# Second attention of a two-block transformer kernel: normalised weights, value products by feature, rounding straight from PSUM

## The chip, the cores and the metric

One NeuronCore of a Trainium2 chip runs the whole program in one launch. The metric is device time in microseconds (us), the median of the runs. Three runs of the kernel before took 1004.45, 1004.01 and 1004.02 us.

## The reference

Two transformer blocks run one after the other on 256 tokens of width 1024, all in float32. The first has an FFN, a mixer of two attentions, and another FFN. The second has an HGRN2 mixer beside a softmax attention of 8 heads of 128 features (called MoBA; with 256 tokens there is a single block, so it is plain causal attention with a relative bias), then a merge of the two branches, an output projection and an FFN. The change touches this attention alone. What it computes, for each head:

```
lo = einsum('bhqd,bhsd->bhqs', qc, ko) * Dh ** -0.5
lo = where(dist_o >= 0, lo + table_h[:, t5_bucket(dist_o)], -inf)
p = softmax(lo, axis=-1)
o = einsum('bhqs,bhsd->bhqd', p, vo)
```

and later `o @ w_branch_attn`, a product over the 1024 features of all heads.

## The kernel before

**Products at full precision.** Every large product with weights is done in a rounded 32-bit format (float32r). Each operand is split into a rounded part (hi) and the rest (lo), and the product is three matmuls: hi by hi, hi by lo, lo by hi (`three`). One such group over 128 rows of the inner dimension is called a tile here: 3 matmuls of 128x512. A `half` is four tiles. A weight piece (128x2048, 1 MB) serves two halves, one for each 128 tokens (t = 0, 1), and PE waits for the piece (`lo_ready`) at the first tile of its first half. A piece takes three steps: two DMAs bring it into one of three slots of `raw`, issued once the lo part of the piece three places before is made; ScalarE (ACT) writes its hi part (`hi`, L1258); VectorE (DVE) writes the lo part by subtraction (`lo`, L1870; `half_lo`, L1876, does it in two instructions, and signals with the second).

**Attention beside a projection.** The second block's projection (36 pieces, `N_WIN2`) is still running when the attention starts. `attention_between` exists once for each engine, and each engine does its own list in order, so the order in the code is the order of the work. Eight heads are taken as four pairs p = 8 to 11. For each pair PE does: `scores` (waits for q, k and `o_out`, the output of the pair before, since scores and outputs share the PSUM tensor `gu`), some tiles of the projection, `turn_weights` (six transposes of the exponentials), more tiles, `weights_read` (waits until the transposed weights are copied to SBUF), `turn_qk` for the next pair, `values`, and the last tiles. `laid` says how many tiles stand in the three places: before the change (4, 1, 2) quarters, which is 8, 2 and 4 tiles.

DVE's list in a pair: `maxima` (adds the bias, finds row maxima), the lo parts of pieces put off, a PSUM evacuation where a block of the projection has ended, `weights_out` (copies the transposed weights), `also` (the gate product of the HGRN2 branch, `gate_of`, for pairs 9 and 10), `k_out`, `output` (four products with the reciprocal of the softmax sum, from PSUM to `proj`), one more lo part. ACT's list: `exps`, hi parts and evacuations, `weights_out`, `q_out`.

**Value products.** The transposed weights are the stationary operand, the values move, and the output has tokens on its partitions (three 128x128 matmuls a head, L948 to L950, each in float32, which the trace records as two matmuls).

**Into operand form.** The product with `w_branch_attn` (T_WAT, four pieces from N_WAT) needs the features on the partitions. So in the stage of the HGRN2 branch product (T_WHG) PE turns the outputs back, 16 transposes in four fills (L654), DVE copies them out (`fill_scaled`, L1888), ACT rounds them (L1268) and DVE subtracts (`fill_rest`, L1896).

Of the kernel before, what the change touches and what calls it, by code (L numbers as in the profile page):

```python
# [7 lines left out]
F32 = mybir.dt.float32  # L8
# [51 lines left out]
TURN_AFTER = {T_WOUT: N_WOUT, T_WAT: N_WHG, T_WOUT2: N_WAT}  # L60
# [15 lines left out]
FOX_LEAD = (3, 3)  # L76
FOX_BEHIND = {4: (1, 2), 5: (1, 2), 6: (1, 1), 7: (0, 0)}
# [46 lines left out]
def build(nc, x_d, wg_d, wu_d, wd_d, win_d, wout_d, win2_d, whg_d, wat_d, wout2_d,  # L124
          fixed_d, rows_d, post_d, rel_d, level_d, hot_d, out_d, row_d, skew_d):

    with ExitStack() as ctx:
# [117 lines left out]
        late_exp, late_rden, o_first = sem("late_exp"), sem("late_rden"), sem("o_first")  # L245
        pT_full, pT_a, pT_d, pv_done, o_out = sem("pT_full"), sem("pT_a"), sem("pT_d"), sem("pv_done"), sem("o_out")
# [93 lines left out]
        def laid(p, q0):  # L340


            behind = (4, 1, 2)
            q = q0 + 2 + sum(behind) * (p % 4)
            out = []
            for n in behind:
                out.append(list(range(q, q + n)))
                q += n
            if p % 4 == 3:
                out[2] = []  # L350
            return out

        def halves(quarters):

            return [q // 2 for q in quarters if q % 2]
# [16 lines left out]
        def fill_bank(u, i):  # L372

            if u == T_WOUT:
                return (gu if i < 2 else acc[:, 1, :, :])[:, i % 2, :]
            return {T_FFN2: acc[:, 1, :, :], T_WHG: acc[:, 1, :, :], T_WAT: gu, T_WOUT2: gu}.get(u, tp)[:, i % 2, :]
# [34 lines left out]
        def turn_n(u):  # L411
            return 4 * u
# [195 lines left out]
        def _(pe):  # L608
# [8 lines left out]
            def half(k, r, banks, j, t, u=None, tiles=range(4), first_j=0, after_first=None):  # L617

                if t == 0 and tiles[0] == 0:
                    pe.wait_ge(lo_ready, k + 1 + 3 * r)  # L620
                w_hi, w_lo = (w.rearrange("p (k n) -> p k n", k=4) for w in split_weights(k))
                for a in tiles:
                    hi, lo = (place[:, a, :] for place in turned_place(u, t, j))
# [19 lines left out]
            def quarters(n0, g0, qs):  # L643
                for q in qs:
                    block_half(n0, g0, q // 2, range(2 * (q % 2), 2 * (q % 2) + 2))
# [447 lines left out]
            def attention_between(p0, n0, g0, h0):  # L1093
# [3 lines left out]
                for p in range(p0, p0 + 4):  # L1097
                    here = laid(p, 2 * h0)
                    scores(p)
                    quarters(n0, g0, here[0])  # L1100
                    turn_weights(p)
                    quarters(n0, g0, here[1])
# [4 lines left out]
                    quarters(n0, g0, here[2])  # L1107
# [99 lines left out]
            for j in range(2):  # L1207
                for t in range(TT):
                    half(N_WHG + 2 + j, 0, acc[:, :, 1, :], j, t, T_WHG)
                    if (j, t) == (0, 1):  # L1210
                        pe.wait_ge(o_out, 12)
                        fills(T_WAT, from_proj(AQ), 0, 1)
                    elif (j, t) == (1, 0):
                        fills(T_WAT, from_proj(AQ), 2, 3)

            filled(T_WAT, 4)
            for j in range(2):
                for t in range(TT):
                    half(N_WAT + j, 0, gu, j, t)
            pe.wait_ge(evac_a, 24)  # L1220
            pe.wait_ge(evac_d, 24)
            for j in range(2):
                for t in range(TT):
# [3 lines left out]
                    half(N_WAT + 2 + j, 0, tp, j, t)  # L1227
# [22 lines left out]
        def _(act):  # L1250
# [164 lines left out]
            def exps(p):  # L1415
# [5 lines left out]
                if pair(p)[0] == 1:  # L1421
                    n = 4 * (p % 2)
                    for r, part in enumerate((late_half, early_half)):
                        cols = slice(S, 3 * P) if r else slice(0, S)
                        for h in range(2):
                            at = 2 * r + h
                            ins = act.activation(e_sb[:, h, cols], part(p, h), ACT.Exp, bias=nmx[:, n + at:n + at + 1],
                                                 accum_out=den[:, at:at + 1])
                        ins.then_inc(exp_done if r else late_exp, 1)
                    return  # L1430
                for h in range(2):
                    lt = late_half(p, h) if p < 8 else src[:, h, 0:S]
                    el = early_half(p, h) if p < 8 else src[:, h, S:3 * P]
# [77 lines left out]

            def attention_between(p0, n0, g0, h0):
# [4 lines left out]
                for p in range(p0, p0 + 4):  # L1517
                    here = [halves(q) for q in laid(p, 2 * h0)]
# [203 lines left out]
            fills(T_WAT, 0, 1, 2, 3)  # L1722
# [134 lines left out]
        def _(dve):  # L1857
# [254 lines left out]
            def weights_out(p):  # L2112
# [8 lines left out]
                reciprocals(p)  # L2121

            def mix(p):

                n = 6 * (p % 2)
                dve.wait_ge(late_exp, p + 1)
                dve.reciprocal(rden[:, n:n + 2], den[:, 0:2]).then_inc(late_rden, 1)
                dve.wait_ge(late_rden, p + 1)
# [111 lines left out]
            def attention_between(p0, n0, g0, h0, also=lambda p: None):  # L2240

                block_out(n0, g0, h0 - 1)
                k_out(p0)
                put_off = [h0 - 1]
                for p in range(p0, p0 + 4):
                    here = [[h for h in halves(q) if h % 2] for q in laid(p, 2 * h0)]
# [13 lines left out]
                    output(p)  # L2260
                    if p < p0 + 3 and put_off:
# [295 lines left out]
            def gate_of(p):  # L2557

                t = p - 8
# [35 lines left out]
            fills(T_WAT, 0, 1, 2, 3)  # L2595
# [84 lines left out]
```

## Time and profile before

| | us |
|---|---|
| median of three runs | 1004.02 |
| the profiled execution, its own time | 1004.47 |
| its span, first to last instruction | 1002.7 |
| PE busy | 997.2 |
| DVE busy | 709.0 |
| ACT busy | 488.2 |

The profile is of one execution. Its page gives busy times, the chain of work that ended last and the costliest groups; the trace behind it gives each instruction in order of time, what ended each wait, and the busy time of any stretch. The engines are PE (matmuls), PEld (loads of the stationary operand), DVE, ACT, POOL and SP. The attention of the change lies between 683 and 746 us of the span, and the products with the two branches' weights between 746 and 790.

### The profile page before, as it was taken

The numbers are of one execution on the slowest core, as the hardware profiler recorded it, in microseconds if no ns is written. First come the engines' busy times: TensorE is split into PE (matmuls) and PEld (weight loads), VectorE is DVE, ScalarE is ACT, GpSimd is POOL, SyncE is SP. The second block draws the span as 40 slices with busy tenths as digits, with TensorE's granted clock in tenths as the row PEclk, the third lists the DMA queues.
The fourth block names the chain that finished last, engine by engine and source line by source line (L and its number), as shares of the span: only waits on it lengthen the run. The fifth ranks groups of instructions, "written<-read, shape, count | busy, mean of one in ns | idle before, by whom it ended". The sixth has DMA issues, their size and how long they took to land.

```text
span 1002.7 us, 14623 instructions
## 1 busy us (share of the span) xinstructions
PE 997.2 (99%) x5311; PEld 838.0 (84%) x5311; DVE 709.0 (71%) x818; ACT 488.2 (49%) x614; POOL 209.9 (21%) x205
## 2 busy tenths in 40 slices
PE   9999999999999999999999999999999999999998
PEld 6888888878888888888888888888888888888887
DVE  5876767775788767666764479876877777666664
ACT  6444444664665544444544455466446445434342
POOL 2232222014100232323010081151000012313230
PEclk9999999999999999999999999999999999999999
DMA  9655656745424655465736545344535556555551
GB/s 301 231 176 186 207 183 204 258 134 182 127 91 162 206 172 209 168 209 167 266 133 209 171 166 166 129 145 149 168 116 180 167 169 222 174 192 192 186 207 43
DMA packets 116937, 178.53 MB, mean 178 GB/s; under 512 B 5792, under 2 KB 73920, under 8 KB 116768
## 3 DMA queue, kind: packets, MB, share of 16 engines
q1 hardware_dynamic: 115952, 174.86, 51.9%
q0 software_dynamic: 640, 1.42, 0.5%
q10 hardware_dynamic: 304, 1.70, 0.5%
q8 instruction: 27, 0.44, 0.2%
q14 instruction: 14, 0.11, 0.0%
HBM read 176.88 MB, written 2.64 MB: 179 GB/s over the span
## 4 chain that ended last, share of the span: by engine, by line
PE 95%; DVE 2%; DMA 1%; SPq 1%; ACT 1%; issue 1%; POOL 0%; DVEq 0%
PE acc L611 11%; PE acc L615 11%; PE acc L614 11%; PE tp L791 10%; PE gu L791 10%; PE gu L794 5%; PE tp L794 5%; PE tp L611 4%; PE tp L615 4%; PE tp L614 4%; PE gu L611 3%; PE gu L615 3%; PE gu L614 3%; PE acc L1056 1%; DMA raw<-in_gate 1%; PE acc L879 1%
## 5 line engine op out<-in xcount | busy, mean ns | idle before, releaser
L1870 DVE TENSOR_TENSOR wlo<-raw,whi 128x2048 fp32r<-128x2048 f32 x144 | 339.8, 2368 | 156.0 <-ACT whi L1258 155.2
L1258 ACT ACTIVATE whi<-raw 128x2048 fp32r<-128x2048 f32 x150 | 285.7, 1907 | 55.4 <-PE acc L615 22.2
L791 PE MATMUL tp<-act_in,whi 128*128 128x512 f32 x432 | 103.0, 391 | 0.0
L791 PE MATMUL gu<-act_in,whi 128*128 128x512 f32 x432 | 102.6, 390 | 0.0
L1778 POOL TENSOR_TENSOR tmp<-tmp 128x256 f32<-128x256 f32 x54 | 41.9, 775 | 280.8 <-DVE tmp L1989 280.8
L791 PEld LDWEIGHTS gu<-act_in,whi 128*128 128x128 f32 x432 | 80.9, 188 | 16.6
L611 PE MATMUL acc<-whi,hT_hi 128*128 128x512 f32 x240 | 94.1, 392 | 0.0
L1780 POOL TENSOR_TENSOR sil<-sil,tmp 128x256 f32<-128x256 f32 x54 | 86.9, 1608 | 34.0 <-ACT sil L1330 34.0
L614 PE MATMUL acc<-wlo,hT_hi 128*128 128x512 f32 x240 | 93.7, 390 | 0.0
L615 PE MATMUL acc<-whi,hT_lo 128*128 128x512 f32 x240 | 93.4, 389 | 0.0
L791 PEld LDWEIGHTS tp<-act_in,whi 128*128 128x128 f32 x432 | 79.7, 188 | 16.2 <-DVE wlo L1870 0.5
L1335 ACT ACTIVATE hT_hi<-hid 128x256 fp32r<-128x256 f32 x54 | 22.2, 417 | 138.3 <-DVE hid L2000 131.1
L611 PE MATMUL tp<-whi,act_in 128*128 128x512 f32 x192 | 76.9, 401 | 0.0
L615 PE MATMUL tp<-whi,act_in 128*128 128x512 f32 x192 | 75.0, 391 | 0.0
L614 PE MATMUL tp<-wlo,act_in 128*128 128x512 f32 x192 | 74.8, 390 | 0.0
L1330 ACT ACTIVATE sil<-tmp 128x256 f32<-128x256 f32 x54 | 22.0, 408 | 106.4 <-POOL tmp L1778 106.4
L611 PE MATMUL acc<-whi,act_in 128*128 128x512 f32 x176 | 71.0, 403 | 0.0
L615 PE MATMUL acc<-whi,act_in 128*128 128x512 f32 x176 | 68.8, 391 | 0.0
L614 PE MATMUL acc<-wlo,act_in 128*128 128x512 f32 x176 | 68.6, 390 | 0.0
L1761 POOL TENSOR_SCALAR ms<-sums 128x1 f32<-128x1 f32 (+2 forms) x20 | 12.6, 630 | 245.7 <-ACT junk L1280 159.5
L794 PEld LDWEIGHTS tp<-act_in,wlo 128*128 128x128 f32 x432 | 55.4, 191 | 2.1
L794 PEld LDWEIGHTS gu<-act_in,wlo 128*128 128x128 f32 x432 | 55.4, 191 | 2.1
(345 smaller groups left out, 1800.5 us busy)
## 6 DMA issues: line engine op xcount, KB each, us to landing
raw<-in_w_in SPq DMA_DIRECT2D x96, 512.0 KB, 4.5
raw<-in_down SPq DMA_DIRECT2D x66, 512.0 KB, 4.1
raw<-in_gate SPq DMA_DIRECT2D x64, 512.0 KB, 4.1
raw<-in_up SPq DMA_DIRECT2D x64, 512.0 KB, 4.7
raw<-in_w_out SPq DMA_DIRECT2D x16, 512.0 KB, 4.7
raw<-in_w_branch_hg SPq DMA_DIRECT2D x8, 512.0 KB, 4.4
raw<-in_w_branch_attn SPq DMA_DIRECT2D x8, 512.0 KB, 4.7
post<-in_post_gains SPq DMA_DIRECT2D x3, 512.0 KB, 5.8
```

Source lines behind the costliest of these rows:

```text
L611: pe.matmul(out, hi, w_hi, start=start, stop=False)
L614: pe.matmul(out, hi, w_lo, start=False, stop=False)
L615: return pe.matmul(out, lo, w_hi, start=False, stop=stop)
L791: pe.matmul(banks[:, a, :], w_hi[:, i, a * P:(a + 1) * P], both, start=i == 0, stop=False)
L794: mm = pe.matmul(banks[:, a, 0:S], w_lo[:, i, a * P:(a + 1) * P], act_in[:, i, 0, :], start=False, stop=i == KT - 1)
L1258: act.activation(split_weights(k)[0], raw[:, k % RING, :], ACT.Copy).then_inc(hi_ready, 1)
L1330: act.activation(sil[:, a, :], gate[:, a, :], ACT.Silu).then_inc(sil_ready, 1)
L1335: act.activation(hT_hi[:, a, :], hid[:, a, :], ACT.Copy).then_inc(hT_hi_ready, 1)
L1761: link(pool.tensor_scalar(ms[:, 0:n], sums[:, col:col + n], inv, EPS, ALU.mult, ALU.add))
L1778: pool.tensor_tensor(gate[:, a, :], gate[:, a, :], row, ALU.mult).then_inc(gate_scaled, 1)
L1780: pool.tensor_tensor(sil[:, a, :], sil[:, a, :], row, ALU.mult).then_inc(sil_scaled, 1)
L1870: dve.tensor_tensor(w_lo, raw[:, k % RING, :], w_hi.bitcast(F32), ALU.subtract).then_inc(lo_ready, 1)
```

## The change

1. ACT's `exps` for these pairs does both heads' late queries (tokens 128 to 255, 256 columns) first and both heads' early ones (128 columns) after, and signals each part.
2. DVE gets `normed_weights`: for the late part a reciprocal and two products of 128x256 in SBUF, for the early part the same with 128x128. It stands after the evacuations and ahead of `weights_out`. The reciprocal in `weights_out` falls away.
3. PE's `turn_weights` waits for `mixed` (once for the late, once for the early part), and places the early block first.
4. `values`: the values are the stationary operand, the weights move. A head takes one matmul of 128x256 and one of 128x128; the output has features on its partitions.
5. The output leaves PSUM as an operand: ACT writes the hi part (`rounded_out`, 128x512, placed after `q_out`), DVE the lo part (`output`, one subtraction of 128x512 in place of four products). They go to the columns that the queries and keys of the same pair held.
6. The four fills of T_WAT fall away on PE, ACT and DVE; its halves take their stationary operand from there (`stationary`).
7. The tiles stand 9, 2, 3 (9, 1, 0 for the last pair) in place of 8, 2, 4.
8. The lo part of the piece that was put off from the pair before is done in two instructions: the first where the whole stood, the second after `output`.
9. `gate_of` comes one pair earlier: its first call before the maxima of pair 8, its second in pair 9.

```diff
@@ constants
+MOBA_BEHIND, MOBA_LAST = (9, 2, 3), (9, 1, 0)
@@ laid
-            behind = (4, 1, 2)
-            q = q0 + 2 + sum(behind) * (p % 4)
+            q = 4 * h0 + 4 + sum(MOBA_BEHIND) * (p % 4)
...
+            for n in MOBA_BEHIND if p % 4 < 3 else MOBA_LAST:
@@ operands
+        def stationary(u, t, j, a):
+            if u == T_WAT:
+                return [place(2 * j + a // 2)[:, a % 2, t * P:(t + 1) * P] for place in (attn_hi, attn_lo)]
+            return [place[:, a, :] for place in turned_place(u, t, j)]
@@ PE turn_weights
+                if pair(p)[0] == 2:
+                    for r, blocks in enumerate(((0, 1), (2,))):
+                        pe.wait_ge(mixed, 2 * mixed_n(p) + r + 1)
+                        for h in range(2):
+                            for n in blocks:
+                                to = (n + 1) % 3 * P
+                                mm = pe.transpose(turned[:, h, to:to + P], e_sb[:, h, n * P:(n + 1) * P], idn)
+                    mm.then_inc(pT_full, 1)
+                    return
@@ PE values
+                    if kind == 2:
+                        o = gu[:, 0, h * S:(h + 1) * S]
+                        pe.matmul(o, v[0], pT_sb[:, h, 0:S], start=True, stop=False, skip_group_check=True)
+                        mm = pe.matmul(o[:, P:S], v[1], pT_sb[:, h, S:3 * P], start=False, stop=True, skip_group_check=True)
+                        continue
@@ PE, products with the branch weights
-                    if (j, t) == (0, 1):
-                        pe.wait_ge(o_out, 12)
-                        fills(T_WAT, from_proj(AQ), 0, 1)
-                    elif (j, t) == (1, 0):
-                        fills(T_WAT, from_proj(AQ), 2, 3)
-            filled(T_WAT, 4)
+            pe.wait_ge(o_out, 12)
-                    half(N_WAT + j, 0, gu, j, t)
+                    half(N_WAT + j, 0, gu, j, t, T_WAT)
@@ ACT
+            def rounded_out(p):
+                act.wait_ge(pv_done, p + 1)
+                act.activation(attn_hi(p - 8), heads(gu[:, 0, :], 2), ACT.Copy).then_inc(attn_hi_ready, 1)
...
                     if p < p0 + 3:
                         q_out(p + 1)
+                    rounded_out(p)
...
-            fills(T_WAT, 0, 1, 2, 3)
@@ DVE
+            def late_reciprocals(p):
+                n = 6 * (p % 2)
+                dve.wait_ge(late_exp, mixed_n(p) + 1)
+                dve.reciprocal(rden[:, n:n + 2], den[:, 0:2]).then_inc(late_rden, 1)
+                dve.wait_ge(late_rden, mixed_n(p) + 1)
+            def normed_weights(p):
+                n = 6 * (p % 2)
+                late_reciprocals(p)
+                for h in range(2):
+                    e = e_sb[:, h, 0:S]
+                    ins = dve.tensor_scalar(e, e, rden[:, n + h:n + h + 1], None, ALU.mult)
+                ins.then_inc(mixed, 1)
+                dve.wait_ge(exp_done, p + 1)
+                dve.reciprocal(rden[:, n + 2:n + 4], den[:, 2:4]).then_inc(rden_ready, 1)
+                dve.wait_ge(rden_ready, p + 1)
+                for h in range(2):
+                    e = e_sb[:, h, S:3 * P]
+                    ins = dve.tensor_scalar(e, e, rden[:, n + 2 + h:n + 3 + h], None, ALU.mult)
+                ins.then_inc(mixed, 1)
@@ DVE output
+                if kind == 2:
+                    dve.wait_ge(attn_hi_ready, i + 1)
+                    dve.tensor_tensor(attn_lo(i), heads(gu[:, 0, :], 2), attn_hi(i).bitcast(F32), ALU.subtract)\
+                       .then_inc(o_out, 1)
+                    return
@@ DVE attention_between
                 k_out(p0)
+                also(p0 - 1)
...
                     maxima(p)
-                    for h in put_off:
-                        next_lo(n0, g0, h)
+                    pieces = [n0 + h // 2 + RING for h in put_off]
+                    for k in pieces:
+                        half_lo(k, 0)
                     for h in here[0]:
                         block_out(n0, g0, h)
                     put_off = here[0] + here[1]
+                    normed_weights(p)
                     weights_out(p)
...
                     output(p)
+                    for k in pieces:
+                        half_lo(k, 1)
...
@@ DVE, later
-            fills(T_WAT, 0, 1, 2, 3)
@@ gate_of
-                t = p - 8
+                t = p - 7
```

## Rows read from the trace of the kernel before

**Rows 1.** The page: busy time, share of the span and instructions of each engine.

```profile
PE 997.2 (99%) x5311; PEld 838.0 (84%) x5311; DVE 709.0 (71%) x818; ACT 488.2 (49%) x614; POOL 209.9 (21%) x205
```

**Rows 2.** PE's longest wait of the whole span; then busy times from 683 to 790 us.

```profile
PE gu L675 <- DVE junk L2311: 1.2, 1, 1.2
...
683.00:790.00 107.00, 107.00 (x554) 90.71 (x553) 76.96 (x103) 55.73 (x76) 0.00 (x0) 1.00 0.45 148
```

**Rows 3.** The timeline (start, duration, engine, line): PE at two places.

```profile
745.79 0.39 PE L611 MATMUL acc<-whi,proj_rounded 128*128 128x512 f32 x1
...
762.12 1.03 PE L654 MATMUL gu<-fixed,proj 128*128 128x128 f32 x8
762.91 0.48 PE L611 MATMUL acc<-whi,proj_rounded 128*128 128x512 f32 x1
763.22 0.40 PE L614 MATMUL acc<-wlo,proj_rounded 128*128 128x512 f32 x1
```

**Rows 4.** The timeline: PE in pair 8, and the scores of pair 9.

```profile
688.10 0.48 PE L611 MATMUL acc<-whi,act_in 128*128 128x512 f32 x1
...
693.68 0.82 PE L936 MATMUL acc<-fixed,att_e 128*128 128x128 f32 x6
...
694.25 0.48 PE L611 MATMUL acc<-whi,act_in 128*128 128x512 f32 x1
...
696.60 0.39 PE L948 MATMUL gu<-proj,att_pT 128*128 128x128 f32 x2
...
697.86 0.47 PE L611 MATMUL acc<-whi,act_in 128*128 128x512 f32 x1
...
699.33 0.40 PE L611 MATMUL tp<-whi,act_in 128*128 128x512 f32 x1
...
700.71 0.59 PE L917 MATMUL gu<-att_k,att_q 128*128 128x256 f32 x2
...
701.93 0.48 PE L611 MATMUL tp<-whi,act_in 128*128 128x512 f32 x1
```

**Rows 5.** The timeline: DVE in pair 8 (idle before it, in brackets).

```profile
688.38 0.76 DVE L2097 SCALAR_TENSOR_TENSOR tmp<-gu,proj 128x256 f32<-128x256 f32 x2 [3.29 <-PE gu L920]
...
690.62 2.28 DVE L1870 TENSOR_TENSOR wlo<-raw,whi 128x2048 fp32r<-128x2048 f32 x1
...
698.14 1.13 DVE L2160 TENSOR_SCALAR proj<-gu,rden 128x128 f32<-128x128 f32 x4 [0.59 <-PE gu L950]
...
701.38 0.74 DVE L2051 TENSOR_SCALAR proj<-acc,rstd 128x512 f32<-128x512 f32 x1
```

**Rows 6.** The timeline: ACT in pairs 8 and 11, and PE's values of pair 11.

```profile
690.75 0.51 ACT L1435 ACTIVATE att_e<-tmp,nmx 128x256 f32<-128x256 f32 x1 [3.92 <-DVE nmx L2110]
...
696.80 0.69 ACT L1412 ACTIVATE att_q<-acc,fixed 128x512 f32<-128x512 f32 x1 [1.78 <-PE acc L879]
...
734.57 1.90 ACT L1258 ACTIVATE whi<-raw 128x2048 fp32r<-128x2048 f32 x1
736.38 0.47 ACT L1446 ACTIVATE att_pT<-acc 128x384 f32<-128x384 f32 x1
...
737.20 0.38 PE L948 MATMUL gu<-proj,att_pT 128*128 128x128 f32 x2
```

**Rows 7.** Groups of DVE instructions by shape: count, busy us, mean ns, idle before.

```profile
L1896 DVE TENSOR_TENSOR act_in<-tmp,act_in 128x512 fp32r<-128x512 f32 x26 | 17.7, 690 | 11.7 <-ACT act_in L1268 11.6
...
L1876 DVE TENSOR_TENSOR wlo<-raw,whi 128x1024 fp32r<-128x1024 f32 x12 | 14.5, 1217 | 0.0
...
L2563 DVE TENSOR_TENSOR proj<-proj 128x1024 f32<-128x1024 f32 x2 | 2.4, 1194 | 0.0
...
L2140 DVE SCALAR_TENSOR_TENSOR att_e<-att_e,rden 128x256 f32<-128x256 f32 x4 | 1.9, 486 | 0.1
...
L2170 DVE TENSOR_SCALAR proj<-proj,rstd 128x128 f32<-128x128 f32 x8 | 1.8, 279 | 0.0
...
L2127 DVE RECIPROCAL rden<-den 128x2 f32<-128x2 f32 x4 | 0.7, 162 | 1.1 <-ACT att_e L1427 1.1
```

More of the change, by code:

```diff
@@ L59 @@
 T_FFN1, T_WIN, T_WOUT, T_FFN2, T_WIN2, T_WHG, T_WAT, T_WOUT2, T_FFN3 = range(9)
-TURN_AFTER = {T_WOUT: N_WOUT, T_WAT: N_WHG, T_WOUT2: N_WAT}
+TURN_AFTER = {T_WOUT: N_WOUT, T_WOUT2: N_WAT}
 BY_TILE, BY_HALF = [(0, 0), (0, 1), (1, 0), (1, 1)], [(0, 0), (1, 0), (0, 1), (1, 1)]
@@ L245, in build @@
         late_exp, late_rden, o_first = sem("late_exp"), sem("late_rden"), sem("o_first")
+        attn_hi_ready = sem("attn_hi_ready")
         pT_full, pT_a, pT_d, pv_done, o_out = sem("pT_full"), sem("pT_a"), sem("pT_d"), sem("pv_done"), sem("o_out")
@@ L338, in total, with laid, halves, mixed_n @@
             return wout_banks(b)[:, t, :] if m == 1 else acc[:, t, b, :]
-        def laid(p, q0):
-            behind = (4, 1, 2)
-            q = q0 + 2 + sum(behind) * (p % 4)
+        def laid(p, h0):
+            q = 4 * h0 + 4 + sum(MOBA_BEHIND) * (p % 4)
             out = []
-            for n in behind:
+            for n in MOBA_BEHIND if p % 4 < 3 else MOBA_LAST:
                 out.append(list(range(q, q + n)))
                 q += n
-            if p % 4 == 3:
-                out[2] = []
-            return out
-        def halves(quarters):
-            return [q // 2 for q in quarters if q % 2]
+            return out
+        def halves(tiles):
+            return [q // 4 for q in tiles if q % 4 == 3]
+        def mixed_n(p):
+            return p - (4 if p >= 8 else 0)
+        def attn_hi(i):
+            return proj_rounded[:, :, AQ + i * S:AQ + (i + 1) * S]
+        def attn_lo(i):
+            return proj_rounded[:, :, AK + i * S:AK + (i + 1) * S]
         def logits(p):
@@ L375, in fill_bank @@
                 return (gu if i < 2 else acc[:, 1, :, :])[:, i % 2, :]
-            return {T_FFN2: acc[:, 1, :, :], T_WHG: acc[:, 1, :, :], T_WAT: gu, T_WOUT2: gu}.get(u, tp)[:, i % 2, :]
+            return {T_FFN2: acc[:, 1, :, :], T_WHG: acc[:, 1, :, :], T_WOUT2: gu}.get(u, tp)[:, i % 2, :]
         def first_bank(i, a):
@@ L622, in half @@
                 for a in tiles:
-                    hi, lo = (place[:, a, :] for place in turned_place(u, t, j))
+                    hi, lo = stationary(u, t, j, a)
                     mm = three(banks[:, t, :], hi, lo,
@@ L641, in block_half, with tiles_of @@
                 half(n0 + h // 2, 0, block_banks(g), h // 2 % 2, h % 2, tiles=tiles)
-            def quarters(n0, g0, qs):
+            def tiles_of(n0, g0, qs):
                 for q in qs:
-                    block_half(n0, g0, q // 2, range(2 * (q % 2), 2 * (q % 2) + 2))
+                    block_half(n0, g0, q // 4, [q % 4])
             def fill(u, i, src):
@@ L1097, in attention_between @@
                 for p in range(p0, p0 + 4):
-                    here = laid(p, 2 * h0)
+                    here = laid(p, h0)
                     scores(p)
-                    quarters(n0, g0, here[0])
+                    tiles_of(n0, g0, here[0])
                     turn_weights(p)
-                    quarters(n0, g0, here[1])
+                    tiles_of(n0, g0, here[1])
                     weights_read(p)
@@ L1106, in attention_between @@
                     values(p)
-                    quarters(n0, g0, here[2])
+                    tiles_of(n0, g0, here[2])
             first_block()
@@ L1226, in _ @@
                         fills(T_WOUT2, from_proj(HI), 0, 1)
-                    half(N_WAT + 2 + j, 0, tp, j, t)
+                    half(N_WAT + 2 + j, 0, tp, j, t, T_WAT)
             pe.wait_ge(merged, 2 * TT)
@@ L1420, in exps @@
                 src = logits(p)
-                if pair(p)[0] == 1:
+                if pair(p)[0]:
                     n = 4 * (p % 2)
@@ L1426, in exps @@
                             at = 2 * r + h
-                            ins = act.activation(e_sb[:, h, cols], part(p, h), ACT.Exp, bias=nmx[:, n + at:n + at + 1],
-                                                 accum_out=den[:, at:at + 1])
+                            ins = act.activation(e_sb[:, h, cols], part(p, h) if p < 8 else src[:, h, cols], ACT.Exp,
+                                                 bias=nmx[:, n + at:n + at + 1], accum_out=den[:, at:at + 1])
                         ins.then_inc(exp_done if r else late_exp, 1)
@@ L1517, in attention_between @@
                 for p in range(p0, p0 + 4):
-                    here = [halves(q) for q in laid(p, 2 * h0)]
+                    here = [halves(q) for q in laid(p, h0)]
                     exps(p)
@@ L2120, in weights_out @@
                 dve.tensor_copy(pT_sb[:, 1, :], turned[:, 1, 0:3 * P]).then_inc(pT_d, 1)
-                reciprocals(p)
+                if pair(p)[0] == 0:
+                    reciprocals(p)
+            def late_reciprocals(p):
[17 more added lines that the diff above has]
+                ins.then_inc(mixed, 1)
             def mix(p):
                 n = 6 * (p % 2)
-                dve.wait_ge(late_exp, p + 1)
-                dve.reciprocal(rden[:, n:n + 2], den[:, 0:2]).then_inc(late_rden, 1)
-                dve.wait_ge(late_rden, p + 1)
+                late_reciprocals(p)
                 mix_rows(n + 4, den[:, 0:1], rden[:, n + 1:n + 2], slice(0, S), 2 * p + 1)
@@ L2243, in attention_between @@
                 k_out(p0)
+                also(p0 - 1)
                 put_off = [h0 - 1]
                 for p in range(p0, p0 + 4):
-                    here = [[h for h in halves(q) if h % 2] for q in laid(p, 2 * h0)]
+                    here = [[h for h in halves(q) if h % 2] for q in laid(p, h0)]
                     maxima(p)
-                    for h in put_off:
-                        next_lo(n0, g0, h)
+                    pieces = [n0 + h // 2 + RING for h in put_off]
+                    for k in pieces:
+                        half_lo(k, 0)
                     for h in here[0]:
```

5 lines of the change are left out of this document (2 added, 3 removed).

## The prediction

> **What bounds the kernel now.** I read the page's busy times first: PE is busy for 997.2 us of a span of 1002.7 [rows 1]. Then PE's waits over the whole span: the longest is 1.2 us, at the start, and from 683 to 790 us, where every edit lies, PE is busy for 107.00 of 107.00 us at a granted clock of 1.00, with DVE at 76.96 and ACT at 55.73 [rows 2]. So PE's queue is the time. A PE instruction removed is gained in full unless a wait takes its place, and any wait for DVE or ACT is lost in full. The third view is the timeline of PE, DVE and ACT in this stretch, since the question is whether each result is there when PE comes to it.
>
> **What PE no longer does.** The fills of T_WAT: 16 transposes in two groups of 8. One group starts at 762.12 and the next product at 762.91, and that product's follower comes after 0.31 us where 0.23 is the pace, so a group costs 0.79 + 0.08 = 0.87 us, two cost 1.75 [rows 3]. No PE wait is there to come back [rows 2]. The value products of a pair: six 128x128 matmuls from 696.60 to 697.86, 1.26 us [rows 4]. The new form, 128x256 and 128x128 for each of two heads, is the shape of the scores, 700.71 to 701.93 = 1.22 us [rows 4]. Fewer instructions, then, but as many columns: 0.04 a pair, 0.15 in all. Transposes, tiles and places between them stay equal in number. Together PE loses 1.9 us of work.
>
> **What DVE and ACT do otherwise.** DVE for each pair: the lo part of the output, one 128x512 at 0.69 [rows 7], for four products of 1.13 [rows 5]; and the normalisation. A 128x128 product in SBUF is 0.28, a reciprocal 0.16 [rows 7]. The 128x256 product in SBUF is in no row: the two-input form of that size bounds it above at 0.49, the 128x128 below at 0.28 [rows 7]. I take 0.37, near the one-input row. With about 0.03 us between dependent instructions the normalisation takes 2 x 0.2 + 2 x 0.29 + 2 x 0.2 = 1.4 us of DVE. The Trainium skill's page "VectorE: DVE Perf Modes", section "The perf-mode tier table", has float32 products with a scalar at twice the rate where both sides lie in SBUF. By that the 128x256 would take 0.28 + 0.07 = 0.35, an estimate, and the sum below would fall by under 0.1. ACT gains one rounding of 128x512 per pair, 0.69 as `q_out` of that size [rows 6]. The first gate product (two 128x1024, the first 1.19 [rows 7], so 2.3 with overlap) goes into DVE's 3.29 us of idle before the maxima of pair 8 [rows 5] and costs nothing; were that idle gone, it would cost the maxima up to 2.3. The removed fills free 5 us of DVE and 2.4 of ACT in a stage where neither holds PE, worth nothing.
>
> **Where PE will wait.** I walked the three queues instruction by instruction with the rows' durations: a tile 0.68 (0.77 right after transposes or float32 products, 697.86 to 699.33 being 0.77 + 0.70 [rows 4]), 0.28 us from a PE group's end to DVE's or ACT's start (697.86 to 698.14 [rows 4, 5]), 0.1 from a DVE end to PE, which no row shows (zero to 0.2), and 0.08 of overlap between neighbours on DVE and ACT (734.57 + 1.90 against 736.38 [rows 6]). Done so for the kernel before, the walk puts the scores of pair 9 at 700.75, where the row has 700.71 [rows 4], and finds no wait. For the kernel after it finds three.
>
> *Pair 8, the second half of a lo part.* The put-off piece is 30 of the projection, used from half 60, tile 240. Before, its lo part ran whole from 690.62 [rows 5] and PE came to that tile at 699.33 [rows 4]. Now its second instruction stands behind `output`, which waits for ACT's rounding, which waits for the values. And tile 240 still stands in the third place of pair 8 (tiles 239, 240, 241), ahead of the next scores. Nine tiles in place of eight let the values end 0.7 later, at 698.5. From there: 0.28 + 0.69 (ACT) + 0.04 + 0.61 (lo of the output) + 1.22 (second half lo [rows 7]) + 0.14 = 701.5. PE comes to tile 240 one tile (0.77) after the values, at 699.3. It waits 2.2 us. Behind that tile are queued two tiles and the scores of pair 9, so everything moves. The next load into that slot is issued 8.5 us later than before; its piece (33) isn't touched by ACT until 711.7, so that is hidden.
>
> In pair 9 the piece is 32, first used by tile 256, after the scores of pair 10; these wait for the same output, and take as long (1.22) as the half lo. No wait, though only 0.1 to 0.6 us is left.
>
> *Pair 10, the chain to the transposes.* After the output of pair 9 DVE has the half lo, a whole lo (2.28) and an evacuation (0.74) ahead of the maxima [rows 5, 7]: 716.2 to 720.2, while the scores end at 717.9. Maxima 2.24 (688.38 to 690.62 [rows 5]), 0.13 to ACT, two exponentials of 0.5 [rows 6], reciprocal and two products: the late weights are ready at 724.5. PE has nine tiles, 6.3 us, and is there at 724.2: it waits 0.4, and 0.2 more for the early weights. Before, eight tiles (688.10 to 693.68 [rows 4]) were more than enough, since exponentials were all.
>
> *Pair 11, ACT's order.* ACT's `weights_out` stands behind the exponentials, an evacuation and a hi part (1.90). Before, it started at 736.38, right behind that hi part, and PE's values at 737.20 [rows 6], so its slack was about 0.3 us. Now the maxima are held by half a lo and a whole one (733.9, scores done at 732.3), the exponentials start at 736.2, the copy at 740.4, and is read at 741.0. PE is there at 739.9: it waits 1.1.
>
> **Sum.** 2.2 + 0.6 + 1.1 = 3.9 us of waits, less 1.9 of work: 2.0 us longer. From the profiled execution's 1004.47 that is 1006.5; the median of the runs is 0.45 lower, so 1006.0. With the 128x256 product at 0.49 the waits grow to 4.0, at 0.28 they fall to 3.7. With half a microsecond either way for the second and the third, which hang on slacks of tenths, the case spans 1005.2 to 1007.0.
>
> **Rivals.** (a) *The waits are covered and the removed work is the result:* 1004.0 - 1.9 = 1002.1, faster. It would need the 2.2 us of pair 8 to vanish, so that the lo part of piece 30 is ready by 699.3; it decides where values, rounding and subtraction together take under 0.8 us, and rows 5 to 7 have 1.3 for the last two alone. Against it, then, is nearly everything; for it, that PE has not waited once here [rows 2], so slacks may be longer than my tenths. (b) *Only the wait in pair 8 comes:* 2.2 - 1.9 = +0.3, 1004.3. Pairs 10 and 11 hang on 0.4 to 1.1 us after long chains, and any of them may be shorter. (c) *The chain grows:* the scores of pair 10 and piece 32 are also within 0.6 us, and each pair's lateness is handed on through DVE, whose queue is full in pairs 9 and 10. Another 1.5 to 2 us: 1008. (d) *PE's clock falls behind the wait.* Rows have a clock of 1.00, the 2.4 GHz level, through this stretch, with no idle in it [rows 2]; a PE idle of 2.2 us in mid kernel is in no row, the longest at the start being 1.2. At 1.2 GHz the fourteen tiles of one pair would take 9.5 us more (14 x 0.68): up to 1015. The Trainium skill's page "TensorE: Matmul & The Clock Gate", section "HAM oscillation — how this bites in real kernels", says idle gaps that are long enough put the clock back to half. The trace agrees as far as it goes.
>
> **How the numbers follow.** The forecast with three waits 0.57, (a) 0.08, (b) 0.20, (c) 0.12, (d) 0.03. A measurement here tells from no change what is over about 0.2%, 2 us. The forecast's own range lies half over 1006.03 and half under, so: slower 0.29 + 0.12 + 0.03 and a little of what I have not seen, 0.48; same 0.28 + 0.20 less a little, 0.43; faster 0.09. The range from 1002.8 to 1007.8 leaves out (a), (d) and the far part of (c).
>
> **What would show it.** In the profile after: a PE wait of about 2 us near 699.3, at the first `tp` tile after the values of pair 8, released by the half lo part on DVE; the transposes of pair 10 waiting for a DVE product on `att_e`; the values of pair 11 waiting for ACT's `att_pT`; values of a pair 1.2 us long; 16 fewer transposes; the granted clock at 1.00. The forecast is wrong if the first is absent, or if the first product with `w_branch_hg` (745.79 before [rows 3]) doesn't come 3.3 to 4.5 us later.

## The result, and the profile after

The kernel after takes 1006.05 us (median of 20 runs, 1005.53 to 1007.74), the kernel before 1004.01 (20 runs, 1003.78 to 1004.45). The ratio of the means is 1.0024, 95% interval 1.0017 to 1.0030. So the change makes the kernel slower, by 2.0 us between the medians.

The 20 runs of after stand in two groups: 11 at a mean granted clock of 1.000, 1005.53 to 1006.07 with a mean of 1005.86, and 9 at 0.998, 1006.96 to 1007.74 with a mean of 1007.23. None of the 69 runs of the kernel before whose clock is on record (those beside the experiments) is below 1.000, and the longest of its 20 runs here took 1004.45. The profiled execution took 1006.01, its span is 1004.2, and it belongs to the first group. It has to be read against the profiled 1004.47 of before: 1.54 longer.

The busy times of the page answer to [rows 1]: 32 matmul records fewer, 0.5 us less of busy PE, a longer span.

```profile
PE 996.7 (99%) x5279; PEld 836.4 (83%) x5279; DVE 708.2 (71%) x821; ACT 488.2 (49%) x614; POOL 209.3 (21%) x205
```

PE's waits over the whole span (total, times, longest) answer to [rows 2]. Two are new, each happens once, and the wait of 1.2 at the start is the old one.

```profile
PE tp L628 <- DVE wlo L1906: 1.9, 1, 1.9
PE gu L692 <- DVE junk L2373: 1.2, 1, 1.2
PE gu L975 <- ACT att_pT L1471: 0.7, 1, 0.7
```

The busy times from 683 to 790 us (PE, PEld, DVE, ACT, POOL, then the clock) show 2.74 of idle PE where there was none, at a granted clock of 1.00. This is less than the delay below: idle time counts from the modelled end of the last product, some 0.17 after the next one was due, and what is held inside a group of transposes doesn't count as idle at all. Where this text says that a group of products ends, it means the start of the product behind it, as the prediction does.

```profile
683.00:790.00 107.00, 104.26 (x515) 86.87 (x514) 74.08 (x105) 53.98 (x76) 0.00 (x0) 1.00 0.46 148
```

**Pair 8.** PE's timeline, for [rows 4] (in brackets the idle before, and what ended it):

```profile
697.79 0.60 PE L975 MATMUL gu<-att_pT,proj 128*128 128x256 f32 x2
698.22 0.38 PE L976 MATMUL gu<-att_pT,proj 128*128 128x128 f32 x2
698.36 0.48 PE L628 MATMUL acc<-whi,act_in 128*128 128x512 f32 x1
...
701.24 0.47 PE L628 MATMUL tp<-whi,act_in 128*128 128x512 f32 x1 [1.93 <-DVE wlo L1906]
```

ACT's and DVE's timelines of the same moment, for [rows 5, 6]:

```profile
698.64 0.60 ACT L1540 ACTIVATE proj_rounded<-gu 128x512 fp32r<-128x512 f32 x1 [0.62 <-PE gu L976]
```

```profile
691.93 0.62 DVE L2167 TENSOR_SCALAR att_e<-att_e,rden 128x256 f32<-128x256 f32 x2
...
699.27 0.69 DVE L2205 TENSOR_TENSOR proj_rounded<-gu,proj_rounded 128x512 fp32r<-128x512 f32 x1 [1.19 <-ACT proj_rounded L1540]
699.88 1.22 DVE L1906 TENSOR_TENSOR wlo<-raw,whi 128x1024 fp32r<-128x1024 f32 x1
```

These rows are one chain: the values end at 698.36; ACT rounds (698.64); DVE subtracts (699.27) and only then makes the second half of the lo part of piece 30 (699.88 to 701.10); tile 240 starts at 701.24. Tile 239 began at 698.36 and would have let it start 0.77 later, at 699.13. So it comes 2.1 late. The products of tile 240 itself take 0.08 more than the pace (701.24 to 702.00 by the same timeline, 0.76 where a tile takes 0.68), so the place costs 2.2 in all.

**Pairs 10 and 11.** PE at the two places, then DVE in pair 10 and ACT in pair 11:

```profile
723.72 0.39 PE L632 MATMUL acc<-whi,act_in 128*128 128x512 f32 x1
724.18 1.07 PE L956 MATMUL acc<-fixed,att_e 128*128 128x128 f32 x6
...
738.24 0.82 PE L956 MATMUL acc<-fixed,att_e 128*128 128x128 f32 x6
...
740.49 0.70 PE L975 MATMUL gu<-att_pT,proj 128*128 128x256 f32 x2 [0.73 <-ACT att_pT L1471]
```

```profile
723.51 0.62 DVE L2167 TENSOR_SCALAR att_e<-att_e,rden 128x256 f32<-128x256 f32 x2
...
724.28 0.48 DVE L2174 TENSOR_SCALAR att_e<-att_e,rden 128x128 f32<-128x128 f32 x2
```

```profile
738.16 1.90 ACT L1284 ACTIVATE whi<-raw 128x2048 fp32r<-128x2048 f32 x1
739.96 0.47 ACT L1471 ACTIVATE att_pT<-acc 128x384 f32<-128x384 f32 x1
```

In pair 10 the transposes are due at 723.95 (723.72 + 0.23) and start at 724.18, when the late weights have just been made (723.51 + 0.62 = 724.13); and the group is 1.07 long where pair 11's is 0.82, since the early weights are made only at 724.76. Together 0.5. The view of waits has no row for this one, so a missing row doesn't mean that nothing waits for some tenths. In pair 11 the values are due 0.57 of transposes and 0.77 of a tile after 738.24: at 739.58. They start at 740.49, 0.9 late, behind a copy that stands behind a hi part; and the first of them takes 0.70 where the others take 0.60, so 1.0 in all.

**Behind them.** The first WHG product [rows 3] and the first WAT product:

```profile
749.15 0.39 PE L628 MATMUL acc<-whi,proj_rounded 128*128 128x512 f32 x1
...
770.91 0.39 PE L628 MATMUL gu<-whi,proj_rounded 128*128 128x512 f32 x1
```

The first comes 3.36 later than the 745.79 of before; the second 1.54 later than before's 769.37. So between them the kernel gains 1.82, the four fills. Counted from where pair 8's queries are turned (683.26 before, 683.12 after), the first comes 3.50 later.

### The profile page after: what moved, and what is told of

It is laid out like the page before. It is cut to its first block, busy times and chain, and to the rows that moved or that the text cites. A ratio compares the mean times of both kernels' runs of the same rounds, so it can differ in the third digit from the quotient of the medians.

```text
span 1004.2 us, 14552 instructions
## 1 busy us (share of the span) xinstructions
PE 996.7 (99%) x5279; PEld 836.4 (83%) x5279; DVE 708.2 (71%) x821; ACT 488.2 (49%) x614; POOL 209.3 (21%) x205
## 4 chain that ended last, share of the span: by engine, by line
PE 94%; DVE 3%; ACT 1%; issue 1%; POOL 0%; DVEq 0%; ACTq 0%
PE acc L628 11%; PE acc L631 11%; PE acc L632 11%; PE tp L808 10%; PE gu L808 10%; PE gu L811 5%; PE tp L811 5%; PE tp L628 4%; PE tp L632 4%; PE tp L631 4%; PE gu L628 3%; PE gu L631 3%; PE gu L632 3%; PE acc L1087 1%; PE acc L896 1%
## 5 line engine op out<-in xcount | busy, mean ns | idle before, releaser
L1900 DVE TENSOR_TENSOR wlo<-raw,whi 128x2048 fp32r<-128x2048 f32 x141 | 332.7, 2367 | 157.7 <-ACT whi L1284 156.8
L1808 POOL TENSOR_TENSOR tmp<-tmp 128x256 f32<-128x256 f32 x54 | 39.8, 737 | 281.6 <-DVE tmp L2019 281.6
L628 PE MATMUL tp<-whi,act_in 128*128 128x512 f32 x176 | 70.6, 401 | 1.9 <-DVE wlo L1906 1.9
L632 PE MATMUL tp<-whi,act_in 128*128 128x512 f32 x176 | 68.7, 390 | 0.0
L631 PE MATMUL tp<-wlo,act_in 128*128 128x512 f32 x176 | 68.6, 390 | 0.0
```

Of the source, the lines that this page charges most:

```text
L628: pe.matmul(out, hi, w_hi, start=start, stop=False)
L631: pe.matmul(out, hi, w_lo, start=False, stop=False)
L632: return pe.matmul(out, lo, w_hi, start=False, stop=stop)
L1808: pool.tensor_tensor(gate[:, a, :], gate[:, a, :], row, ALU.mult).then_inc(gate_scaled, 1)
L1900: dve.tensor_tensor(w_lo, raw[:, k % RING, :], w_hi.bitcast(F32), ALU.subtract).then_inc(lo_ready, 1)
```

## The experiments

Times are medians. Unless said otherwise the runs are all at a clock of 1.000. The before beside them took 1003.97 (33 runs, with E1 to E4), 1004.01 (27 runs, with E5 to E8) and 1004.17 (9 runs, with E9).

One thing has to be known before times of two traces are compared. Pair 8's queries are turned at 682.5 to 682.8 in some executions (E1, E2, E5 to E9) and at 683.1 to 683.3 in others (before, after, E3, E4). This half microsecond has nothing to do with the edits: it is there within the first 9 us of the span. So the stretch from that turn to the first WHG product is given too, where it says more than the time: 62.53 us before, 66.03 after.

**E1: piece 30 whole again.** The kernel after, with one edit in DVE's list of pair 8.

```diff
+                    whole = pieces if p == p0 else []
+                    pieces = [] if p == p0 else pieces
...
                     weights_out(p)
+                    for k in whole:
+                        lo(k)
```

> The kernel after, with one thing taken back: the lo part of piece 30, in pair 8, is done in one instruction behind DVE's weights_out, where DVE is idle for 1.7 us, instead of half of it behind output. Theory (the wait at tile 240 is that half instruction standing behind the rounding): the PE wait of 1.9 us near 699 is gone, tile 240 starts one tile (0.78) after the values, the waits of pairs 10 and 11 (0.5 and 1.0 us) stay as they are, and the time falls by 2.1 us, from 1005.9 to 1003.8. Rival (DVE's full queue in pairs 9 and 10 is the bound, the wait in pair 8 only shows it early): the time comes back as longer waits in pairs 10 and 11, fall under 1 us. On the clock: of 20 runs of the kernel after, 12 had a mean granted clock of 1.000 and took 1005.5 to 1006.1, 8 had 0.998 and took 1007.0 to 1007.7, none of the 20 before had 0.998. If the long wait is what makes the clock fall, no run of this kernel has 0.998.

(The two groups count 11 and 9, not 12 and 8.) Measured 1003.42 (11 runs, 1003.15 to 1003.99), ratio 0.9994 [0.9985, 1.0003]. That is 2.4 under the mean of after's full-clock runs; the stretch from the turn of pair 8's queries to the first WHG product is 63.86, 2.2 shorter. Its timeline of PE shows three tiles in a row behind the values, with nothing between them:

```profile
697.88 0.48 PE L628 MATMUL acc<-whi,act_in 128*128 128x512 f32 x1
...
698.66 0.39 PE L628 MATMUL tp<-whi,act_in 128*128 128x512 f32 x1
```

while its waits still hold the one of pair 11, 0.7, and its transposes in pair 10 still take 1.08. So the place of half an instruction is worth more than the whole net loss, and theory and size hold.

**E2: ACT copies the weights first in pair 11.**

```diff
                     exps(p)
+                    if p == p0 + 3:
+                        weights_out(p)
...
-                    weights_out(p)
+                    if p < p0 + 3:
+                        weights_out(p)
```

> The kernel after, with ACT's weights_out of pair 11 put ahead of the evacuation and the hi part that stood in front of it. Theory (the wait of pair 11 is ACT's order): the wait of PE's values for att_pT falls from 0.7 in the trace (1.0 with the restart) to about 0.2, time 0.8 us less, 1005.1. Rival (DVE's late normalisation holds pair 11 whatever ACT does): no change, 1005.9. The wait near 699 stays, and with it some runs at a clock of 0.998.

Measured 1006.36, ratio 1.0018 [1.0009, 1.0027], in two groups: 5 runs at 1.000 with a mean of 1005.23, 6 at 0.998 with a mean of 1006.45. At the full clock that is 0.63 less than after's 1005.86, near the 0.73 of the wait row, which is gone; the values still start 0.17 after they are due. The median missed, because more than half of the runs were at the lower clock. Its profiled execution is one of these, and shows how that looks (granted clock in the third last column):

```profile
697.00:700.00 3.00, 1.71 (x10) 1.18 (x8) 1.81 (x3) 2.27 (x4) 0.00 (x0) 1.00 0.00 0
700.00:703.00 3.00, 2.36 (x7) 1.96 (x8) 3.00 (x3) 1.24 (x1) 0.00 (x0) 0.74 0.37 72
703.00:706.00 3.00, 3.00 (x13) 2.47 (x12) 1.12 (x4) 0.00 (x0) 0.00 (x0) 0.69 1.04 395
706.00:709.00 3.00, 3.00 (x15) 2.49 (x14) 2.86 (x7) 1.39 (x6) 0.00 (x0) 1.00 0.62 232
```

```profile
700.64 0.47 PE L628 MATMUL tp<-whi,act_in 128*128 128x512 f32 x1 [1.93 <-DVE wlo L1909]
...
701.41 0.60 PE L628 MATMUL tp<-whi,act_in 128*128 128x512 f32 x1
701.80 0.63 PE L631 MATMUL tp<-wlo,act_in 128*128 128x512 f32 x1
702.23 0.63 PE L632 MATMUL tp<-whi,act_in 128*128 128x512 f32 x1
702.65 1.05 PE L934 MATMUL gu<-att_k,att_q 128*128 128x256 f32 x2
...
704.96 0.48 PE L628 MATMUL tp<-whi,act_in 128*128 128x512 f32 x1
```

Products that come every 0.23 us come every 0.43 from 701.8 on, and the pace is back at 704.96: from tile 240 to there is 4.32, in the trace of after 2.67 (701.24 to 703.91). The clock was at the 1.2 GHz level for some 3 us. In this trace it cost 1.65; the groups' means are 1.2 apart.

**E3: all three waits removed by order alone.** The kernel after with E1's and E2's edits; the split kept for pair 9 only, so that the lo part of piece 34 in pair 10 is also made whole, behind DVE's `weights_out`; the whole lo part of piece 33, which stood ahead of the maxima of pair 10, made behind them (`held`); and eight tiles in place of nine ahead of the last pair's transposes.

```diff
-MOBA_BEHIND, MOBA_LAST = (9, 2, 3), (9, 1, 0)
+MOBA_BEHIND, MOBA_LAST = (9, 2, 3), (8, 2, 0)
...
+                    split = pieces if p == p0 + 1 else []
+                    whole = [] if p == p0 + 1 else pieces
...
+                    if p == p0 + 2:
+                        lo(held)
```

> The kernel after, with four moves and no work changed: piece 30 and piece 34 whole behind weights_out; piece 33 whole behind the maxima of pair 10 instead of ahead of them; ACT's weights_out of pair 11 ahead of its evacuation and hi part; the last pair's tiles 8 and 2 instead of 9 and 1. Theory (the waits are queue positions, and the work removed from PE, 1.9 us, is gained in full once they are gone): no PE wait from 683 to 790 us, the first product with w_branch_hg near 745.5 of the span, time 1004.0 - 1.9 = 1002.1, all clocks 1.000. Rival (DVE lacks time for the normalisation beside the projection, however ordered): at least one wait of half a microsecond or more is left and the time stays over 1002.8.

Measured 1002.12 (11 runs, 1001.71 to 1002.97), ratio 0.9982 [0.9973, 0.9991]: faster than both kernels. The busy times show the stretch whole again, and the timeline has the first WHG product 0.2 ahead of the 745.79 of before (0.13 of it since the turn of pair 8's queries, which is the gain of the value products):

```profile
683.00:790.00 107.00, 107.00 (x531) 90.15 (x529) 77.27 (x105) 55.66 (x76) 0.00 (x0) 1.00 0.46 148
```

```profile
745.58 0.39 PE L628 MATMUL acc<-whi,proj_rounded 128*128 128x512 f32 x1
```

This is the removed work of 1.9 with no wait, the figure of rival (a).

**E4: the split alone, on the kernel before.**

```diff
-                    for h in put_off:
-                        next_lo(n0, g0, h)
+                    pieces = [n0 + h // 2 + RING for h in put_off]
+                    for k in pieces:
+                        half_lo(k, 0)
...
                     output(p)
+                    for k in pieces:
+                        half_lo(k, 1)
```

> The kernel before, with one part of the change alone: the put-off lo part is done in two instructions, the second behind output (still four products, no rounding by ACT, no normalisation). Theory: the split alone makes PE wait at tile 240. The values end at 697.86, then 0.28 + 1.05 (output) + 1.22 (second half) + 0.14 = 700.5 against 699.33: a wait of 1.2 us, and 0.1 in pair 11, so 1005.3. Rival (it is the rounding by ACT that makes the wait; the split is hidden without it): no wait, 1004.0. On the clock: with a wait of 1.2 us, no longer than one that the kernel before has at its start, I expect 1.000 in all runs.

Measured 1005.75 (11 runs, 1005.31 to 1005.93), ratio 1.0016 [1.0007, 1.0025], 0.5 over the expectation. Tile 240 waits here too:

```profile
700.58 0.47 PE L611 MATMUL tp<-whi,act_in 128*128 128x512 f32 x1 [1.05 <-DVE wlo L1876]
```

It comes 1.25 after the 699.33 of before [rows 4], and the first WHG product 1.45 after the 745.79, 0.04 of which was there before the attention. The means of the runs are 1.58 apart, the medians 1.78; the 0.2 to 0.4 over 1.41 is in no row of these two traces, and stays open. The split is harmful by itself: tile 240 is 1.2 late here. With E7 below, where the ninth tile is taken back and it is 1.4 late, the 2.1 of the change comes apart into 1.2 for the split, 0.2 for the rounding in the chain and 0.7 for the ninth tile that delays the values.

**E5: the fills gone, nothing else.** The kernel before. It leaves out the turning and rounding of this attention's output.

```diff
-TURN_AFTER = {T_WOUT: N_WOUT, T_WAT: N_WHG, T_WOUT2: N_WAT}
+TURN_AFTER = {T_WOUT: N_WOUT, T_WOUT2: N_WAT}
...
-                        fills(T_WAT, from_proj(AQ), 0, 1)
```

> The kernel before without the four fills between the WOUT products and without the work on DVE that turned the attention output: its halves are read from what act_in held before, so the turning and rounding of the second attention's output is left out, and nothing takes its place. My theory: TensorE loses four fills of 128x512 in the two places of the product phase, 1.75 by the rows of the fills (0.87 each pair), and no wait is added or removed in pairs 8 to 11: 1002.2 against 1004.0, and the first WAT product about 1.8 earlier. Rival: the fills stood where TensorE waits anyway or where the products behind them make the time up; then 1003.5 to 1004.0. A second rival: the first WAT products now find weights or their operand late, and the gain is partly a wait of its own, 1003 or so, with a wait row at the first WAT product.

(The fills stand between the WHG products; the expectation's "WOUT" is a slip.) Measured 1002.36 (11 runs, 1001.96 to 1002.69), ratio 0.9983 [0.9974, 0.9992]: 1.65 between the medians and 1.76 between the means, for the 1.75. The first WAT product is at 767.05 for 769.37; 0.50 of these 2.32 were there when pair 8's queries were turned (682.76 for 683.26), so the fills account for 1.82. They were work in full.

**E6: the wait doubled.** The kernel after, in pair 8 alone:

```diff
-                        half_lo(k, 0)
+                        if p > p0:
+                            half_lo(k, 0)
...
+                        for _ in range(2 if p == p0 else 0):
+                            link(half_lo(k, 0))
                         half_lo(k, 1)
```

> The kernel after, but in pair 8 alone the half lo of piece 30 is put behind the output and done twice, linked, so that tile 240's wait grows from 1.9 to about 4.6 us. It asks whether the length of this wait decides if the granted clock falls behind it. The changed kernel ran at a mean clock of 1.000 in 11 of 20 runs and at 0.998 in 9, about 1.2 us longer; with the wait at 1.0 (E4) or gone (E1, E3) none of 33 runs did. Theory A, the wait's length matters and longer is worse: the time is 1006.0 + 2.6 = 1008.6 where the clock holds, and the clock falls behind the wait in all or nearly all runs: median 1009.8 or more. Theory B, the fall is a matter of the wait's place alone: again about half of the runs at 0.998, median 1008.6 to 1009.8 in two groups. Theory C, the 0.998 belongs to this chip's moment and not to the wait: groups that don't follow the kernel, and the fast one at 1008.6.

Measured 1010.21 (5 runs, 1010.00 to 1010.91), ratio 1.0063 [1.0049, 1.0076]; every run is at 0.997 or 0.998. Theory A. The wait is 4.45, 2.5 more than in after, which makes 1008.4 at the full clock; the other 1.8 is the clock's (2.16 in the trace: from tile 240 to the first product behind the scores it is 4.83, in after 2.67). The first product behind the wait is slow already, and the granted clock is low in each of the stretches from 700 to 709, in the first of which PE does nothing:

```profile
703.30 0.77 PE L628 MATMUL tp<-whi,act_in 128*128 128x512 f32 x1 [4.45 <-DVE wlo L1906]
703.87 0.63 PE L631 MATMUL tp<-wlo,act_in 128*128 128x512 f32 x1
```

```profile
700.00:703.00 3.00, 0.00 (x0) 0.00 (x0) 2.93 (x3) 1.38 (x1) 0.00 (x0) 0.67 0.01 3
703.00:706.00 3.00, 2.69 (x6) 2.15 (x7) 3.00 (x3) 0.00 (x0) 0.00 (x0) 0.50 0.48 108
706.00:709.00 3.00, 3.00 (x13) 2.57 (x12) 0.61 (x3) 0.00 (x0) 0.00 (x0) 0.69 1.05 402
```

**E7: the tiles as before.** The kernel after with `(8, 2, 4), (8, 2, 0)`. (What moves is a tile, 0.68, and not a fill, as the expectation has it.)

> The kernel after with the tiles of the MOBA turns given out as before, eight and two with four behind, in place of nine with three behind. It moves one fill of 128x512 (0.47) out of the stretch ahead of the wait in pair 8. My theory: the wait at the late tile shrinks, because what DVE does for it stands further from TensorE: by the walk of the queues waits of 1.4, 0.5 and 0.3 are left in pairs 8, 10 and 11, in place of 1.9, 0.5 and 1.0: 1.4 less than 1006.0 at full clock, 1004.6. Rival: the ninth tile covers the normalisation of the weights on DVE, and without it TensorE waits at the values in each pair, 0.3 to 0.5 in each of four: 1006.5 to 1008.

Measured 1004.36 (11 runs, 1004.15 to 1004.94), ratio 1.0004 [0.9995, 1.0013]. That is 1.5 under after's full-clock mean, as the walk had it (1.4): 0.7 of it in pair 8, where the values end a tile earlier, and the rest in pair 11, where two tiles stand between transposes and values and cover ACT's copy. The rival is out: there is no wait row at the values of any pair, and the only one left in the attention is this (the 0.5 of pair 10, which has no row, is there as well: its transposes take 1.08):

```profile
PE tp L628 <- DVE wlo L1906: 1.2, 1, 1.2
```

**E8: the gate back.** The kernel after, `also(p0 - 1)` taken out and `t = p - 8`.

> The kernel after with the work of the gate at the places that it had before the change (behind the pair, not ahead of it). My theory: the gate's place has no part in the 2.0 us; DVE had 0.9 idle ahead of pair 8's first piece: the same waits at tile 240, in pair 10 and in pair 11, 1006.0 (1005.6 at full clock, some runs at 0.998 and 1007). Rival 1: the gate in front of pair 8 is what makes DVE late, and with it back the wait of 1.9 shrinks by its 1.2: 1004.8. Rival 2: the gate put back falls into pair 10's and 11's crowded DVE and lengthens their waits by 0.5 to 1: 1006.8.

Measured 1005.85 (11 runs), ratio 1.0020 [1.0011, 1.0029]: 8 runs at 1.000 (1005.45 to 1006.22), 3 at 0.998 (1006.98 to 1007.35). Its waits are those of after, 1.9 and 0.7. The stretch from the turn of pair 8's queries to the first WHG product is 66.04, after's to 0.01. The gate has no part in it; DVE's idle ahead of the maxima of pair 8 is 3.29 again, in after 0.90.

**E9: a wait of 2.3 without the change.** E4 with the first half of piece 30 done once more in pair 8, behind `output`.

```diff
                     for k in pieces:
+                        if p == p0:
+                            link(half_lo(k, 0))
                         half_lo(k, 1)
```

> The kernel before with the split of E4 alone, and in pair 8 the first half lo of piece 30 done twice, linked: one more half of 1.22 on DVE (its row in E4's trace) makes E4's wait of 1.05 at tile 240 some 2.3. Nothing else of the change is in it. It asks whether the granted clock's fall belongs to the length of the wait or to the change's new products. So far: waits of 1.94 and less than 2.0 in three kernels with the new products gave 18 of 42 runs at a mean clock of 0.997 to 0.998; 4.45 gave 5 of 5; 1.24 and less gave none of 44. Theory A, length: at the full clock 1005.6 + 1.3 = 1006.9, and half or more of the runs at 0.998 and 1.2 longer, so the median is 1006.9 to 1008.1. Theory B, the fall comes with the new value products (their matmuls of 128x128 with fresh weights in front of the wait): no run below 0.999, median 1006.9, all within 0.5 of it.

Measured 1008.11, ratio 1.0035 [1.0021, 1.0049]: 2 runs at 1.000 (1006.74, 1007.33), 3 at 0.998 (1008.11 to 1008.48). The first two are on the 1006.9 expected, the others 1.2 over them: theory A again, though on five runs only. The old value products have the fall too:

```profile
701.14 0.47 PE L611 MATMUL tp<-whi,act_in 128*128 128x512 f32 x1 [2.31 <-DVE wlo L1876]
701.44 0.40 PE L614 MATMUL tp<-wlo,act_in 128*128 128x512 f32 x1
...
702.15 0.63 PE L614 MATMUL tp<-wlo,act_in 128*128 128x512 f32 x1
...
705.77 0.40 PE L614 MATMUL tp<-wlo,act_in 128*128 128x512 f32 x1
```

## Why the prediction was right

**What PE no longer does.** Predicted 1.75 for the fills: 1.82 between the two traces, 1.65 to 1.82 by E5. Predicted 0.04 a pair for the value products: from 697.13 to 698.36 they take 1.23 in pair 8, for 1.26.

**What DVE and ACT do.** The 128x256 product in SBUF, which no row had, takes 0.35 (a pair of them 0.62), where I took 0.37. The estimate that the prediction worked out from the Trainium skill's double rate ("VectorE: DVE Perf Modes", section "The perf-mode tier table") was 0.35; the trace agrees. The rounding takes 0.60, not 0.69: I had read it from `q_out`, which also scales. The gate is hidden (E8).

**Pair 8.** Predicted 2.2 at tile 240; it is 2.1, and the chain is the one that was walked, shorter by the 0.09 of the rounding. E1 took it out and gave back 2.4 (2.2 between the traces, counted from the turn of pair 8's queries). The step that no row of before showed, from DVE's end to PE, is 0.14 (699.88 + 1.22 to 701.24); the prediction names it as 0.1 and has 0.14 in this sum.

**Pairs 10 and 11.** Predicted 0.6 and 1.1; measured 0.5 and 1.0. The sign named for pair 10, transposes that wait for a DVE product, is there in the times and not as a row of the waits. E2 took out the second and gave back 0.63. E1 and E2 together give back 2.4 + 0.6 = 3.1, the 2.1 + 1.0 that the trace has for the two; E3 gives back all three, 1005.86 - 1002.12 = 3.7 for 3.6.

**The sum.** 2.1 + 0.5 + 1.0 = 3.6 of waits less 1.95 of work is 1.65; the two profiled executions differ by 1.54, and the new one had run 0.14 ahead before the attention began (683.12 for 683.26 at the turn of pair 8's queries), which makes 1.68. The first WHG product came 3.36 later, just inside the 3.3 to 4.5 that were named. The mean of the full-clock runs is 1.78 over the mean of before. The forecast was 2.0, each of its three waits being 0.1 too long, and that the medians are 2.04 apart is in part luck: some 0.2 to 0.3 of that comes from the runs with a fallen clock, which the sum had not.

**Rival (d)** was the one half seen. I gave it 0.03 and up to 9.5 us, a clock down for a whole pair. It came in 9 of 20 runs and cost 1.4; in the trace that shows it, E2's, the clock was low for some 3 us. So the chance was far too low and the price far too high, and the granted clock of 1.00, which the prediction named among its signs, held in 11 of 20 runs only. The Trainium skill ("TensorE: Matmul & The Clock Gate", section "HAM oscillation — how this bites in real kernels") has idle gaps as the cause; the traces agree in kind, though a single idle of 1.93 us, shorter than those of the page's case, did it here.

**The others.** (a) is what E3 makes of the change. (b) would have needed pairs 10 and 11 to be better by 1.5. (c) did not come: the scores of pair 10 follow the tile before them at the pace of 0.23 (716.24, 716.47).

## What to carry to other kernels

When one engine is never idle, price an edit by the queue order of the engines that feed it: what stands in front of each operand that it needs next, and how many of its own instructions are still between. Work that is cut in two to let something else pass must have its second half placed by the first use of the result, not by convenience; here one half instruction behind a three-step chain cost more than four removed fills gave. Moving a filler tile ahead of a late product moves every result behind that product too, and takes it from where it covered a copy (E7: some 0.7 us for each).

## What the hardware showed that was not expected

A single idle of PE of about 2 us, in a stretch where it is otherwise busy throughout, lowers the granted clock in some executions of one and the same program and not in others (the wait is that of each kernel's trace):

| PE's wait in pair 8 | kernels | runs below 0.999 |
|---|---|---|
| none to 1.24 | E1, E3, E4, E7 | 0 of 44 |
| 1.93 to 1.94 | after, E2, E8 | 18 of 42 |
| 2.31 | E9 | 3 of 5 |
| 4.45 | E6 | 5 of 5 |

Between groups of one kernel the price is 1.2 to 1.4 us; in the traces it is 1.65 (E2), 1.59 (E9, from tile 240 to the first product behind the scores, against E4) and 2.16 (E6). E9 shows that the wait alone does it, without the new products. The chip is not what makes the groups: E1 to E4 ran on one, with 0 of 33 runs below 0.999 for E1, E3 and E4 and 6 of 11 for E2; E5 to E8 on another, with none of 11 for E7 and 5 of 5 for E6.

Where the clock falls differs too. In E6 it falls within the idle, at 701.0, with PE idle since 698.9 and until 703.3; in E2 at 701.4, 0.8 us after the products have begun again; in E9 at 702.1, 1.0 after (worked out from the mean clocks of half microseconds, the third last column; first E6, then E2 twice, then E9).

```profile
701.00:701.50 0.50, 0.00 (x0) 0.00 (x0) 0.50 (x1) 0.38 (x1) 0.00 (x0) 0.50 0.00 0
```

```profile
701.00:701.50 0.50, 0.50 (x4) 0.42 (x3) 0.50 (x1) 0.24 (x1) 0.00 (x0) 0.93 0.00 0
701.50:702.00 0.50, 0.50 (x3) 0.40 (x2) 0.50 (x1) 0.00 (x0) 0.00 (x0) 0.50 0.67 74
```

```profile
702.00:702.50 0.50, 0.50 (x3) 0.43 (x2) 0.50 (x1) 0.00 (x0) 0.00 (x0) 0.59 0.98 61
```

What decides in a single run is open: in the traces of E2 and E8 PE's products start within 0.01 us of each other from 682.5 to the end of a wait of 1.93 and 1.94, and the clock falls in E2 alone.
